# Block 1's routed experts: one step per expert, token rows of 4 KB and four weight places in place of 64-token blocks, rows of 2 KB and three places

## The reference, cut to what matters

```python
scores = sigmoid(xt @ w_router)                  # 512 tokens x 64 experts
sel = lax.top_k(cand, 8)[1]                      # cand: biased scores of the 4 best groups of 8 experts
wts = take_along_axis(scores, sel, 1); wts = wts / wts.sum(-1) * 2.5
def expert_block(args):                          # xe: tokens of one expert, e: which
    xe, e = args
    return (silu(xe @ w_gate_l[e]) * (xe @ w_up_l[e])) @ w_down_l[e]
routed = segment_sum(yb * slot_w[:, None], slot_tok)[:t]
shared = (silu(xt @ w_sh_gate) * (xt @ w_sh_up)) @ w_sh_down
return routed + shared
```

## Time and profile before

| | us |
|---|---|
| median of 3 runs | 3191.98 |
| lowest, highest | 3186.73, 3194.73 |
| the profiled execution, its own time | 3193.44 |
| its span, first to last instruction | 3191.7 |
| mean granted TensorE clock | 0.942 of full speed |
| PE busy | 2779.7 (87% of the span) |
| PE weight loads | 1338.4 (42%) |
| DVE, ACT, POOL busy | 929.3, 460.0, 501.5 (29%, 14%, 16%) |
| moved by DMA | 792.94 MB, 248 GB/s in the mean |

### The profile page before, as it was taken

One profiled execution on the slowest core, in us unless ns is written; L12 is line 12 of the kernel. 1 busy time (PEld: TensorE's weight loads), 2 busy tenths in 40 slices (PEclk: granted clock), 3 DMA queues, 4 the chain that ended last, 5 costly groups with the idle time before them and its releaser, 6 DMA issues.

```text
span 3191.7 us, 36733 instructions
## 1 busy us (share of the span) xinstructions
PE 2779.7 (87%) x15269; PEld 1338.4 (42%) x15269; DVE 929.3 (29%) x1541; ACT 460.0 (14%) x1007; POOL 501.5 (16%) x383
## 2 busy tenths in 40 slices
PE   5999699989989899988999498685998898888887
PEld 2644566744435454444445233443332232223232
DVE  2043556531123511111111476843111111111112
ACT  2011233201012111111111201430000000000001
POOL 0001134312001133433434101301000000000000
PEclk8899899989989999999999799797999999999999
DMA  5020154442122599997999420034999999999996
GB/s 229 27 79 0 55 160 148 146 155 104 75 95 104 194 351 387 370 364 286 361 371 371 145 89 23 24 146 159 421 421 421 421 421 421 421 421 421 422 421 286
DMA packets 127325, 792.94 MB, mean 248 GB/s; under 512 B 21795, under 2 KB 22179, under 8 KB 56761
## 3 DMA queue, kind: packets, MB, share of 16 engines
q1 hardware_dynamic: 102328, 743.86, 57.9%
q0 software_dynamic: 23008, 37.81, 4.9%
q10 hardware_dynamic: 1824, 8.91, 0.7%
HBM read 768.91 MB, written 38.86 MB: 253 GB/s over the span
## 4 chain that ended last, share of the span: by engine, by line
PE 55%; DMA 28%; DVE 9%; issue 4%; ACT 3%; POOL 1%; ACTq 0%; POOLq 0%; SPq 0%; DVEq 0%
DMA arena<-in_w_down 12%; PE b L2991 10%; DMA yd<-arena 9%; PE b L1452 5%; PE b L1888 4%; PE b L492 4%; DMA arena<-h2d,arena 3%; PE b L3026 3%; PE b L494 3%; PE b L2479 2%; PE b L1902 2%; PE b L633 2%; PE b L1516 2%; PE b L1470 2%; DVE arena L2525 2%
## 5 line engine op out<-in xcount | busy, mean ns | idle before, releaser
L2991 PE MATMUL b<-arena 128*64 128x512 f32 x2048 | 457.6, 604 | 18.1 <-DMA arena<-in_w_up 7.8
L1888 PE MATMUL b<-arena 128*64 128x256 f32 x3072 | 356.4, 384 | 5.4 <-DMA arena<-in_w_gu 4.2
L3006 PE MATMUL b<-arena 128*64 128x512 f32 x1024 | 244.2, 602 | 57.2 <-DMA arena<-in_w_down 57.0
L2991 PEld LDWEIGHTS b<-arena 128*64 128x64 f32 x2048 | 156.0, 139 | 315.9 <-issue 276.6
L1888 PEld LDWEIGHTS b<-arena 128*64 128x64 f32 x3072 | 213.5, 137 | 117.2 <-issue 5.4
L2205 POOL DMA_INDIRECT yd<-arena x96 | 152.5, 1588 | 344.8 <-ACT arena L1986 113.7
L1902 PE MATMUL b<-arena 128*64 128x512 f32 x768 | 187.1, 608 | 0.9 <-issue 0.7
L2161 DVE TENSOR_TENSOR arena<-arena,b 128x128 f32<-128x128 f32 x96 | 27.8, 290 | 519.7 <-ACT arena L1979 481.9
L1452 PE MATMUL b<-arena 128*128 128x512 f32 x384 | 167.0, 596 | 9.1 <-DMA arena<-in_w_in 9.1
L3006 PEld LDWEIGHTS b<-arena 128*64 128x64 f32 x1024 | 65.0, 136 | 235.8 <-DMA arena<-in_w_down 136.2
L3098 DVE TENSOR_TENSOR arena<-arena,b 128x512 f32<-128x512 f32 x32 | 20.6, 686 | 463.7 <-PE b L2991 463.7
(11 more groups left out here) (479 smaller groups left out, 3382.7 us busy)
## 6 DMA issues: line engine op xcount, KB each, us to landing
arena<-in_w_gu SPq DMA_DIRECT2D x65, 2048.0 KB, 9.7
arena<-in_w_gate SPq DMA_DIRECT2D x128, 1024.0 KB, 27.0
arena<-in_w_up SPq DMA_DIRECT2D x128, 1024.0 KB, 26.1
arena<-in_w_down SPq DMA_DIRECT2D x128, 1024.0 KB, 24.5
arena<-in_w_dn SPq DMA_DIRECT2D x65, 1024.0 KB, 11.9
arena<-in_w_mod SPq DMA_DIRECT2D x80, 512.0 KB, 3.7
arena<-in_w_in SPq DMA_DIRECT2D x19, 2048.0 KB, 8.0
arena<-yd SPq DMA_DIRECT2D x12, 512.0 KB, 8.6
```

The lines of the kernel that those rows point to most:

```text
L1888: x = e.matmul(ps[i % 2][64 * j:64 * j + 64, 0:256], XGT[i % 2][:, k % 4, (k // 4) * 64:(k // 4) * 64 + 64], GUB[place_of(w)][:, k, j * 25 ...
L2991: x = e.matmul(ps[b + c][64 * hf:64 * hf + 64, :], XS[q % 2][:, kb, (n % 2) * 64:(n % 2) * 64 + 64], w[:, u * 512:(u + 1) * 512], start=(k ...
L3006: x = e.matmul(ps[4][64 * hf:64 * hf + 64, :], H[:, c * 4 + j, hi * 64:hi * 64 + 64], w[:, i * 1024 + hf * 512:i * 1024 + hf * 512 + 512], ...
```

## The change

Each expert is one step, 64 in all (`N` = 64). A step is whole if its expert is one of the 32 largest (`whole(i)`), and then takes its 128 slots at once with products on the whole array: the tokens are 128 columns of weights, the up products move 512 columns, the down products 512. Small experts stay at 64 tokens with products in pairs of half arrays. Tokens are moved as whole rows of 1024 numbers, 4 KB: a whole step gathers and scatters 128 rows, a half step 64. Upper and lower slots of a large expert come from its two columns (the last table product places them), so the row number is the token's own (`tok1`, -1). Transposes of tokens are eight in either kind: of 128 columns in a whole step, of 64 rows in a half step. A whole step uses banks 6 and 7 for one step's tokens and banks 4 and 5 for one step's output, where two blocks alternated. There are four token buffers and gathers four steps ahead, three output buffers, four weight places, and the fourth lies over the one-hot tables and their scratch. The loop over overflow comes ahead of step 33 and POOL enters it two steps earlier. The number of sums stays three.

The diff, cut to its core:

```diff
-    t["below"] = np.broadcast_to(np.where(r >= 64, 0.0, -1.0), (128, 1))
-    t["odd"] = 2 * (r + 128 * np.arange(4)[None, :]) + 1
+    t["tok1"] = r + 128 * np.arange(4)[None, :] + 1
...
-        self.yd = [dram(f"yd{i}", [1024, 512], F32) for i in range(3)]
+        self.yd = [dram(f"yd{i}", [512, 1024], F32) for i in range(3)]
...
-MID = 48
+MID = 33
+SUMS = 3
...
+    PPf, TMP = ar(4096), ar(2048)
+    GUB.append(PPf.rearrange("p (k n) -> p k n", k=8))
+    DNB.append(TMP.rearrange("p (k n) -> p k n", k=2))
...
-    Y = [rows(512) for _ in range(4)]
+    Y = [rows(1024) for _ in range(3)]
+    XG = [under(1024), under(1024), under(1024), XGf[:, 0:1024]]
...
-    order = [0, *range(1, blocks[MID][0]), None, *range(blocks[MID][0], 65)]
+    N = 64
+    order = [*range(MID), None, *range(MID, N)]
+    def whole(i):
+        return ranks[i] < RANKS2
     def place_of(w):
-        return (number[w] + 2) % 3
+        return number[w] % 4
     def freed(e, n, kind):
+        if n == 2:
+            e.wait_ge(*mm.at("s_" + kind, 3))
+        elif n == 3:
+            e.wait_ge(*mm.at("table", 31))
+        elif n > 3 and order[n - 4] is None:
             e.wait_ge(o["end"], 16)
+        elif n > 3:
+            e.wait_ge(*mm.at(kind, order[n - 4]))
...
+    def gate_up(e, i):
+        g = GUB[place_of(i)]
+        e.wait_ge(*came_gu[place_of(i)].at(i))
+        e.wait_ge(*dve.at("xt", i))
+        if i >= 2:
+            e.wait_ge(*dve.at("hid", i - 2))
+        for k in range(8):
+            if whole(i):
+                x = e.matmul(ps[i % 2][:, :], XGT[i % 2][:, hs(k)], g[:, k, :], start=(k == 0), stop=(k == 7))
+                continue
+            for j in range(2):
+                x = e.matmul(ps[i % 2][64 * j:64 * j + 64, 0:256], XGT[i % 2][:, k * 64:k * 64 + 64],
+                             g[:, k, j * 256:(j + 1) * 256], start=(k == 0), stop=(k == 7), skip_group_check=True)
+    def down(e, q):
+        e.wait_ge(*act_.at("hidT", q))
+        if q >= 1:
+            e.wait_ge(*act_.at("y", q - 1))
+        for j in range(2):
+            for c in range(2):
+                if whole(q):
+                    x = e.matmul(ps[4 + c][:, :], HDT[q % 2][:, hs(j)], d[:, j, c * 512:(c + 1) * 512], start=(j == 0), stop=(j == 1))
+                else:
+                    x = e.matmul(ps[4][64 * c:64 * c + 64, :], HDT[q % 2][:, 64 * j:64 * j + 64],
+                                 d[:, j, c * 512:(c + 1) * 512], start=(j == 0), stop=(j == 1), skip_group_check=True)
...
     def tokens_T(e, i):
-        e.wait_ge(*came_xg[i % 6].at(i))
-        if i >= 2:
-            e.wait_ge(*dve.at("xt", i - 2))
-        for c in range(4):
-            x = e.transpose(p[:, hs(c)], XG[i % 6][:, hs(c)], K.ident)
+        e.wait_ge(*came_xg[i % 4].at(i))
+        if i:
+            e.wait_ge(*dve.at("xt", i - 1))
+        for k in range(8):
+            if whole(i):
+                x = e.transpose(ps[6 + k // 4][:, hs(k % 4)], XG[i % 4][:, hs(k)], K.ident)
+            else:
+                x = e.transpose(ps[6][:, k * 64:k * 64 + 64], XG[i % 4][0:64, hs(k)], K.ident[0:64, 0:64])
...
+    def weighted(e, q):
+        r, y = ranks[q], Y[q % 3]
+        e.wait_ge(*mm.at("dn", q))
+        if q >= 3:
+            e.wait_ge(*yout[q % 3].at(q - 3))
+        for c in range(2):
+            rs = slice(64 * c, 64 * c + 64)
+            dst, src, w = (y, ps[4 + c], WS) if whole(q) else (y[0:64], ps[4][rs], WS[rs])
+            x = e.activation(dst[:, c * 512:(c + 1) * 512], src[:, :], ACT.Copy, scale=w[:, r:r + 1])
...
+        if whole(i):
+            e.tensor_copy(XGT[i % 2][:, 0:512], ps[6][:, :]).then_inc(*dve.up("xt0", i))
+            e.tensor_copy(XGT[i % 2][:, 512:1024], ps[7][:, :]).then_inc(*dve.up("xt", i))
         else:
-        e.tensor_copy(XGT[i % 2], heads(ps[6 + i % 2][:, :])).then_inc(*dve.up("xt", i))
+            e.tensor_copy(XGT[i % 2][:, 0:512], ps[6][:, :]).then_inc(*dve.up("xt", i))
...
     def gather(e, i):
         if i < N:
-            if i >= 6:
-                e.wait_ge(*mm.at("xt", i - 6))
-            e.indirect_dma_start(XG[i % 6], None, K.h2d2, off(GI.bitcast(U32)[:, b:b + 1]), bounds_check=1023,
+            if i >= 4:
+                e.wait_ge(*mm.at("xt", i - 4))
+            e.indirect_dma_start(XG[i % 4][rows_of(i), :], None, K.h2d, off(GI.bitcast(U32)[rows_of(i), r:r + 1]), bounds_check=511,
...
-            if i == MID - 3:
-                ov_pool(e, (i - 1) // 3 * 3)
-            gather(e, i + 6)
+            if i == MID - 2:
+                ov_pool(e, (i - 1) // SUMS * SUMS)
+            gather(e, i + 4)
             e.wait_ge(*act_.at("y", i))
-            if i >= 3:
-                e.wait_ge(*yout[(i - 3) % 4].at(i - 3))
-            e.indirect_dma_start(K.yd[i % 3], off(GI.bitcast(U32)[:, b:b + 1]), Y[i % 4], None, bounds_check=1023,
+            if i >= SUMS:
+                e.wait_ge(*yout[(i - SUMS) % 3].at(i - SUMS))
+            e.indirect_dma_start(K.yd[i % SUMS], off(GI.bitcast(U32)[rows_of(i), r:r + 1]), Y[i % 3][rows_of(i), :], None, bounds_check=511,
```

More of the change, by code:

```diff
@@ L1715, in experts @@
     hi = K.area(K.base1 + 4096, K.keep1)
-    XG = [hi(512) for _ in range(4)]
+    XGf = hi(2048)
     ar = K.area(K.keep1)
@@ L1804, in sp @@
         e.dma_start(rbias, I["rbias"]).then_inc(*came_rb.up())
-        load(e, 0)
+        load_shared(e)
         K.norm2.done(e)
@@ L1822, in sp @@
                 ov_sp(e, n)
-            elif w > 2:
-                if n >= 3 and order[n - 3] is None:
+            elif w > 1:
+                if n > 3 and order[n - 4] is None:
                     ov_end(e)
@@ L1834, in pe @@
         x.then_inc(*mm.up("route"))
-        e.wait_ge(*came_gu[2].at(0))
+        e.wait_ge(*came_gu[2].at("shared"))
         shared_gu(e, 0)
@@ L1873, in pe @@
             for j in range(2):
-                x = e.matmul(ps[7][64 * j:64 * j + 64, u * 160:u * 160 + 160], K.ident[:, 64 * u:64 * u + 64], TB, start=True, stop=True, skip_group_check=True)
+                for lo, n, at in (((0, 160, 0),), ((0, 32, 64), (32, 128, 32)))[j]:
+                    x = e.matmul(ps[7][64 * j:64 * j + 64, u * 160 + lo:u * 160 + lo + n], K.ident[:, 64 * u:64 * u + 64], TB[:, at:at + n],
+                                 start=True, stop=True, skip_group_check=True)
         x.then_inc(*mm.up("table2"))
@@ L1880, in pe @@
             if i < N:
-                w = blocks[i][0]
-                e.wait_ge(*came_gu[place_of(w)].at(w))
-                e.wait_ge(*dve.at("xt", i))
-                if i >= 2:
-                    e.wait_ge(*dve.at("hid", i - 2))
-                for k in range(8):
-                    for j in range(2):
-                        x = e.matmul(ps[i % 2][64 * j:64 * j + 64, 0:256], XGT[i % 2][:, k % 4, (k // 4) * 64:(k // 4) * 64 + 64],
-                                     GUB[place_of(w)][:, k, j * 256:(j + 1) * 256], start=(k == 0), stop=(k == 7), skip_group_check=True)
-                x.then_inc(*mm.up("gu", i))
+                gate_up(e, i)
                 if i + 1 < N:
@@ L1893, in pe @@
             if i > 0:
-                q = i - 1
-                w = blocks[q][0]
-                e.wait_ge(*came_dn[place_of(w)].at(w))
-                e.wait_ge(*act_.at("hidT", q))
-                if q >= 2:
-                    e.wait_ge(*act_.at("y", q - 2))
-                for j in range(2):
-                    for c in range(2):
-                        x = e.matmul(ps[4 + q % 2][64 * c:64 * c + 64, :], HDT[q % 2][:, 64 * j:64 * j + 64],
-                                     DNB[place_of(w)][:, j, c * 512:(c + 1) * 512], start=(j == 0), stop=(j == 1), skip_group_check=True)
-                x.then_inc(*mm.up("dn", q))
+                down(e, i - 1)
             if i < N:
@@ L1927, in shared_y @@
         if n == 0:
-            e.wait_ge(*came_dn[2].at(0))
+            e.wait_ge(*came_dn[2].at("shared"))
         else:
@@ L2146, in place @@
         e.wait_ge(*dve.now())
-        e.scalar_tensor_tensor(out=GI.bitcast(I32), in0=ps[7][:, 0:160], scalar=C["below"], in1=E0, op0=ALU.add, op1=ALU.add).then_inc(*dve.up("slots"))
+        e.scalar_tensor_tensor(out=GI.bitcast(I32), in0=ps[7][:, 0:160], scalar=-1.0, in1=E0, op0=ALU.add, op1=ALU.add).then_inc(*dve.up("slots"))
     def dve_(e):
@@ L2191, in pool @@
         all_of(e, *began, zeroed)
-        for i in range(6):
+        for i in range(4):
             gather(e, i)
@@ L2212, in experts @@
     gcol, wcol = K.tiny(1), K.tiny(1)
[L2213 to L2216 removed]
+    assert not whole(MID)
+    b_gu, b_dn, b_t, b_ht = ps[MID % 2], ps[(MID + 1) % 2], ps[7], ps[2 + MID % 2]
     def more(e):
@@ L2279, in ov_pe @@
             e.wait_ge(o["xg"], i * 16 + 16)
-            for c in range(4):
-                x = e.transpose(b_t[:, hs(c)], xr[:, hs(c)], K.ident)
+            e.transpose(b_t[:, 0:128], K.ident, K.ident)
+            for k in range(8):
```

(3 more changed lines are left out.)

140 lines of the change are left out of this document (69 added, 71 removed).

## The result

The changed kernel takes 3212.96 us (median of 5 runs, 3208.49 to 3219.9) where the kernel before, run beside it, takes 3191.98 (5 runs, 3185.13 to 3198.04). The ratio is 1.007, 95% interval 1.0048 to 1.0091: slower by 0.7%, some 21 us, where 25 us less were forecast. The profiled execution has a span of 3209.7 us against 3191.7.

What follows compares the result with a forecast made beforehand. The prediction took block 1's experts as PE-paced and interrupted by DMA engines near their own limit. Terms -12.5 - 18 + 4 + 1 + 0.7 = -25 us gave 3167 us against the median 3191.98, range 3148 to 3196.

Steps and rivals of the forecast that it cites:

- PE's work: Block 1's experts on PE: shorter products less added transpose time, over 32 pairs of experts, -12.5 us.
- The pair: One whole and one half step of block 1's experts on PE: 18.56 us against 18.95 before.
- the transposes: Token transposes on PE: the half step's eight 1.03 us against 0.59 before, the whole step's eight 1.18.
- Waits: PE's waits in block 1's experts: of 24 us 6 are left, -18 us.
- the price: DMA time for tokens moved as 4 KB rows: 3.2 us per MB, against 4.13 before.
- B: Rival: tokens cost the DMA engines as much as now, because additions make them dear; 3174 to 3191, say 3183; chance 0.20.
- Start: Start of block 1's experts: larger first gather, more transposes and copies at the lower clock, +4 us.
- Loop: Overflow loop: POOL enters behind the output two steps ahead, five more transposes in the round, +1 us.
- End: End of block 1's experts: one more ACT pass ahead of the last scatter, +0.7 us.
- C: Rival: token queue limited by packet count; half the packets leave no wait for tokens; 3156 us; chance 0.15.
- D: Rival: scatters serial three deep, three output buffers, so steps wait for landings; 3277 us; chance 0.12.
- E: Rival: no change; waits move to weights or behind the loop and eat the gain; 3185 to 3200; chance 0.08.

Runs made afterwards that it cites:

- kernels 2: Changed kernel, with every second large expert's full column and every second small expert's tokens put on partitions 64 to 127; 3185.74 us, 0.9979 of the kernel before.
- experiment 5: Changed kernel with both partition swaps, and slots filled in reverse order in every second pair of ranks; 3185.03 us, 0.9974 of the kernel before.
- the ninth, experiment 9: Kernel before with slots reversed in every second pair of ranks and scatters that write without adding; 3158.26 us in one run.
- the sixth: Kernel before with slots filled in reverse order in every second pair of ranks, nothing else changed; 3179.12 us, 0.9953 of the kernel before.
- experiments 4: Changed kernel with scatters that overwrite and do not add; 3170.22 us in one run.
- the seventh kernel: Changed kernel with both partition swaps, slots reversed in every second pair of ranks, and scatters that write without adding; 3158.19 us in one run.

## Why the prediction was wrong

**PE's work: right in sign, too small.** The pair was forecast at 18.56 and took 17.92; -12.5 us should have been -33. The term missized is the transposes. I had put the half step's eight at 1.03, between 0.89 and 1.18; they took 0.64, 0.08 each, below both bounds. 32 times the 0.39 are 12.5 of the 20 us by which the sum was too small, and the whole step's eight are 8 more. The Trainium skill's rule for weight loads (TensorE: Matmul & The Clock Gate, section LDWEIGHTS) gave 0.85, nearer than my middle, but the measured value lies below it too. The whole step's eight took 0.93 in place of 1.18.

**Waits: the step that failed.** "Of the 24 us of waits I leave 6: -18 us" became +29 us of idle and +17 of slower passes, 14 of them at the half clock behind waits. The waits for gathers went, as forecast; those for weights took their place. Two things in the step were wrong.
First, the price. I took 3.2 us per MB of tokens, on the word of block 2's gathers, where nothing is added. It is 3.94. The queue's rows of before could not part gathers from scatters, as the text said; the rows chosen as the nearest were near to the gathers only. But the single packets of the same trace could: 4 KB take 159 ns where they are gathered and 2 x 176 where they are added, a mean of 256 ns on one of sixteen engines, which is 3.9 us per MB for the 4.13 that was read. That asked for no run. And the packets halved for the scatters alone. This is B's reason, and balanced kernels 2 and 5 land at 3185, where B stood (3183).
Second, the balance, which stood nowhere in the prediction. It summed bytes over sixteen engines as if any of them could take any row. The diff shows it in two places: a whole step's upper 64 slots take the second column, which is mostly empty (536 rows in 2048 slots; 16 us), and a half step's transfers touch 64 partitions where all had touched 128 (11 us). No rival had a word of these 27 us, and it took the time from B's place to 3213, outside the range.
With faster PE work the kernel also needs more bytes per us: a mean pair's 7.34 MB in 17.92 us is 410 GB/s, above the mean rate of every kernel from 1130 to 1400 (at most 394, without additions). So the 33 us could hardly be had in full at any price of tokens between those that I weighed; that is an estimate from these two figures.

**Smaller terms.** Start: +4 forecast; the first up product came 3.6 us later, 2.3 of it behind the table products. Loop: +1 forecast, but the wait there fell by 8.2 and PE's stop from 27.0 to 19.6 us, with PE itself later than its transfers. It came back as soon as PE was faster (17.6 in experiment 5). End: from the last down product to the last scatter's issue 2.18 us against 1.48, +0.7 as forecast. I had called the overflow round empty; one expert has 145 tokens, so the round carries 17.

**The rivals.** C fell: a third fewer packets did not free the token queue, whose price per MB went with the bytes that are added. Its premise failed too: a third of the 8804 packets that it counted held 8 bytes or less, and of the others only those of the scatters halved. By the rule that it drew on (the Trainium skill, DMA: Bandwidth & Descriptors, section Queues, rings and completion order) it had put the time at 3156; taking turns by packets may still be how the engines work, no run here shows it or rules it out. D fell: no wait of PE, outside the end of the stage, ended on ACT's output or a scatter. E had the movement right (waits go from tokens to weights), but not its size.

**Left open.** What the slot reversal is worth on top of the swaps; which engines a 64-partition transfer uses; why PE waits 15 to 18 us for the loop's gather in some kernels and 6 to 8 in others (the ninth 7.0, the sixth 15.5, with the same order of work); and, for want of more than one execution each, how much of the 33 us would arrive without additions.

## What to carry to other kernels

Ask of every transfer not only how many bytes but which partitions it touches, and how full they are: two kernels with the same bytes differed by 27 us because rows gathered on one half of the partitions. Price a transfer that adds by rows of one that adds. Where a fault is found in the new form, mend it in the old one too before the two are compared: here the two then came out level. Where two limits lie level, a gain on one is worth what the other allows, so measure the other's ceiling (here both kernels with plain scatters) before counting the gain.

## What the runs showed of the hardware

- An indirect scatter with addition costs the DMA engines about twice as much per byte as a plain one: 327 ns for a packet of 4 KB, where a gather's 4 KB and a plain scatter's take 159 (changed kernel, experiments 4, 7 and 9). Twice 2 KB take 352, so the larger row saves 7%.
- Rows of 2 KB that are gathered, or scattered without addition, moved in packets of 4 KB; only scatters with addition moved in packets of 2 KB (8192 of them before, none of the stage's 96 scatters in experiment 9).
- A third fewer token packets with the same bytes changed the queue's price by 5% (4.13 to 3.94 us per MB; 2.56 and 2.69 without additions).
- A half step's eight transposes (weights of 128 columns on 64 partitions, 64 columns moved) take 0.08 us each at the full clock, the whole step's (128 partitions, 128 columns moved) 0.116.
- The half clock behind short waits adds up, though not every wait brings it. Of the 25 whole up products that waited for weights eight took 8.6 to 8.8 us in place of 7.03, behind waits of 1.87 to 3.83 us; the one behind the wait of 3.85 us at 1273.85 took 7.13. Over the stage the 512 records of whole up products were busy 243.8 us with 47.0 us of waits for weights among them; in the seventh kernel, with 6.3, the same records took 14 us less (its group, columns as above):

```profile
L1919 PE MATMUL b<-arena 128*128 128x512 f32 x512 | 229.8, 602 | 7.9 <-DMA arena<-in_w_gu 6.3 <-DVE arena L2227 1.5
```
